# Wide operands in the first two feed-forwards of a four-layer transformer kernel, with a third of their weight splits on GpSimd

## The reference

```python
def conv_ffn(h, w_up, w_conv, w_down):
    gu = causal_dwconv(h @ w_up, w_conv)
    g, u = jnp.split(gu, 2, axis=-1)
    return (jax.nn.silu(g) * u) @ w_down
```

## Time and profile before

| | |
|---|---|
| median of three runs | 1244.94 us (1244.0 to 1245.01) |
| the profiled execution's own time | 1244.72 us |
| its span, first to last instruction | 1243.4 us |
| TensorE (PE) busy | 1228.2 us, 99% |
| VectorE (DVE) busy | 858.4 us, 69% |
| ScalarE (ACT) busy | 622.3 us, 50% |
| GpSimd (POOL) busy | 63.1 us, 5% |
| granted TensorE clock, mean | 0.999 |

### The profile page before, as it was taken

The page is one execution under the profiler, slowest core; times in us unless marked ns, Lnnn a source line. Parts: engine busy times, 40 slices in busy tenths (PEclk is TensorE's granted clock), DMA queues, the critical chain, the costliest instruction groups (busy, mean ns, idle before and its releaser), DMA issues.

```text
span 1243.4 us, 18327 instructions
## 1 busy us (share of the span) xinstructions
PE 1228.2 (99%) x7609; PEld 1085.7 (87%) x7609; DVE 858.4 (69%) x1126; ACT 622.3 (50%) x780; POOL 63.1 (5%) x84
## 2 busy tenths in 40 slices
PE   9999999999999999999999999999999999999997
PEld 8998999988877899988899888888889987888886
DVE  6656877646776787863678787776477567777744
ACT  6536655434556565543575635444326663644430
POOL 0000000000000000000006400000010001000000
PEclk9999999999999999999999999999999999999999
DMA  9654555554533445555443347455536341755530
GB/s 357 242 189 179 186 176 187 196 192 162 194 127 111 186 171 193 179 203 175 162 173 126 137 173 263 175 200 182 176 107 246 106 169 69 270 172 200 173 132 34
DMA packets 32658, 219.25 MB, mean 176 GB/s; under 512 B 3760, under 2 KB 4032, under 8 KB 7616
## 3 DMA queue, kind: packets, MB, share of 16 engines
q1 hardware_dynamic: 30848, 211.80, 47.8%
q0 software_dynamic: 1728, 6.29, 1.4%
HBM read 217.01 MB, written 1.05 MB: 175 GB/s over the span
## 4 chain that ended last, share of the span: by engine, by line
PE 94%; DVE 2%; ACT 2%; DMA 1%; POOL 1%; issue 0%; SPq 0%; DVEq 0%; POOLq 0%
PE ps L873 40%; PE ps L816 11%; PE ps L824 9%; PE ps L828 9%; PE ps L825 9%; PE ps L817 6%; PE ps L818 2%; PE ps L915 1%; PE ps L886 1%; PE ps L925 1%; PE ps L942 1%; DMA t<-in_rows 1%; PE ps L994 0%; DVE t L1413 0%; DMA t<-in_wts 0%; PE ps L1008 0%
## 5 line engine op out<-in xcount | busy, mean ns | idle before, releaser
L873 PE MATMUL ps<-t,t 128*128 128x512 f32 (+2 forms) x2280 | 541.9, 392 | 0.0
L1413 DVE TENSOR_TENSOR t<-t,t 128x2048 fp32r<-128x2048 f32 (+1 forms) x199 | 451.6, 2280 | 118.6 <-PE ps L873 101.5
L873 PEld LDWEIGHTS ps<-t,t 128*128 128x128 f32 x2280 | 417.1, 188 | 84.7 <-issue 1.4
L1117 ACT CAST t<-t 128x2048 fp32r<-128x2048 f32 (+1 forms) x199 | 376.1, 1899 | 226.2 <-PE ps L873 120.7
L824 PE MATMUL ps<-t,t 128*128 128x256 f32 x1024 | 257.7, 284 | 0.0
L825 PE MATMUL ps<-t,t 128*128 128x256 f32 x1024 | 256.6, 283 | 0.0
L816 PE MATMUL ps<-t,t 128*128 128x512 f32 x560 | 201.1, 398 | 0.0
L824 PEld LDWEIGHTS ps<-t,t 128*128 128x128 f32 x1024 | 196.4, 192 | 0.4 <-issue 0.2
L825 PEld LDWEIGHTS ps<-t,t 128*128 128x128 f32 x1024 | 196.4, 192 | 0.2
L817 PE MATMUL ps<-t,t 128*128 128x256 f32 x640 | 166.6, 281 | 0.0
L828 PE MATMUL ps<-t,t 128*128 128x256 f32 x1024 | 164.6, 283 | 0.0
(11 more groups left out here) (201 smaller groups left out, 788.1 us busy)
## 6 DMA issues: line engine op xcount, KB each, us to landing
t<-in_wts SPq DMA_DIRECT2D x195, 1024.0 KB, 4.9
t<-in_rows POOLq DMA_DIRECT2D x12, 512.0 KB, 4.4
t<-in_wts SPq DMA_DIRECT2D x4, 512.0 KB, 5.2
t<-in_wts SPq DMA_DIRECT2D x2, 768.0 KB, 5.0
t<-in_x_in SPq DMA_DIRECT2D x2, 512.0 KB, 4.0
out<-t SPq DMA_DIRECT2D x4, 256.0 KB, 2.1
t<-in_rows SPq DMA_DIRECT2D x2, 256.0 KB, 6.5
t<-in_cst SPq DMA_DIRECT2D x1, 448.0 KB, 13.5
```

The lines of the kernel that those rows point to most:

```text
L873: ins = mm(ps[:, t_bank(stage, t, j), 0:c1 - c0], a, w[:, k, c0:c1], start=kt == 0 and part == 0, stop=kt == KTS[stage] - 1 and part == 2)
L1117: copy(wh[:, k, 0:w], wraw[:, r, 0:w]).then_inc(s_hi, 1)
L1413: tt(wl[:, k, 0:w], wraw[:, r, 0:w], wh[:, h, 0:w].bitcast(F32), ALU.subtract).then_inc(s_lo, 1)
```

## The change

The first two feed-forwards get the wide form too. Three things go with it.

1. `WIDE` now holds all four feed-forwards: 16 matmuls a block, two banks an output, and the matmuls of n+2 wait for `s_wide` of n.
2. The halves are not joined by one reduction. ScalarE copies the half that comes from the low activations into SBUF (`low_half`: 128 x 512 into `XN[:, 1, ...]`, two halves used in turn), and VectorE adds the other half from PSUM to it, in place (`tensor_tensor`). All taps for n >= 2 then read the joined output from SBUF instead of PSUM. ScalarE's copy waits for the matmuls and for the taps of n-2; VectorE's sum for the copy; ScalarE's first tap for the sum.
3. The low split of every third chunk of ffn0 and ffn1 (six in each: places 2, 5, 8, 11, 14, 17 of the 20) is made by GpSimd instead of VectorE (`pool_splits`), with a semaphore of its own; TensorE and SyncE wait for it where they waited for VectorE's.

The order of a step changes with it. Before, step n was: taps n, pump, SiLU or product n. Now it is: copy and sum n, SiLU or product of n-1, pump, taps n.

In the diff the first `lo` is VectorE's and the last GpSimd's; the lines with `s_half_out` and `return` stand in VectorE's `wide_sum`.

```diff
-WIDE = ("ffn2", "ffn3")
+WIDE = HEADED
+def pool_splits(i):
+    return PLAN[i][0] in ("ffn0", "ffn1") and CHUNKS[PLAN[i][0]].index(i) % 3 == 2
...
         for m in done:
             name = "product" if m % 2 else "silu"
-            out += [("conv", q, m)] * (q < 2) + [("wide", q, m)] * (q >= 2 and m > 1) + [("pump",)] * (m == n) + [(name, q, m // 2)]
+            if q >= 2:
+                out += [("wide", q, m)] * (m > 1) + [("pump",)] * (m == n) + [(name, q, m // 2)]
+        if q < 2:
+            late = lambda m: ("product" if m % 2 else "silu", q, m // 2)
+            if n == 2:
+                out += [("conv", q, 0), ("conv", q, 1), late(0), late(1)]
+            out += [("wide", q, n)] + [late(n - 1)] * (n > 2) + [("pump",), ("conv", q, n)] + [late(n)] * (n == 21)
...
+    def lo_ready(i):
+        pooled = sum(pool_splits(n) for n in range(i + 1))
+        return (s_lop, pooled) if pool_splits(i) else (s_lo, split_at(i) - pooled)
...
+    def conv_in(q, n):
+        return ps[:, f_bank(f"ffn{q}", n), :] if n < 2 else XN[:, 1, half_of(n % 2)]
...
         def ffn_conv(q, n):
-            act.wait_ge(*f_done(f"ffn{q}", n))
+            act.wait_ge(*(f_done(f"ffn{q}", n) if n < 2 else wide_at(q, n)))
...
+        def low_half(q, n):
+            bank = f_bank(f"ffn{q}", n)
+            act.wait_ge(*f_done(f"ffn{q}", n))
+            if n >= 4:
+                act.wait_ge(s_cv, 22 * q + n - 1)
+            copy(conv_in(q, n).rearrange("p (a s) -> p a s", a=2), ps[:, bank:bank + 2, S:2 * S]).then_inc(s_half_out, 1)
...
         def lo(i):
-            if i >= len(PLAN):
+            if i >= len(PLAN) or pool_splits(i):
...
             dve.wait_ge(*f_done(stage, n))
+            if q < 2:
+                u = conv_in(q, n).rearrange("p (a s) -> p a s", a=2)
+                dve.wait_ge(s_half_out, 20 * q + n - 1)
+                tt(u, ps[:, bank:bank + 2, 0:S], u, ALU.add).then_inc(s_wide, 1)
+                return
...
+        def lo(i):
+            if i >= len(PLAN) or not pool_splits(i):
+                return
+            w, r, h, k = PLAN[i][5] * PLAN[i][6], i % NRAW, i % NHI, i % NLO
+            pool.wait_ge(*used(i - NLO))
+            pool.wait_ge(s_hi, split_at(i))
+            tt(wl[:, k, 0:w], wraw[:, r, 0:w], wh[:, h, 0:w].bitcast(F32), ALU.subtract).then_inc(s_lop, 1)
```

More of the change, by code:

```diff
@@ L507, in program @@
     s_tap, s_cv, s_silu = sem("s_ffn_tap"), sem("s_ffn_conv"), sem("s_ffn_silu")
-    s_wide = sem("s_ffn_wide_summed")
+    s_wide, s_half_out = sem("s_ffn_wide_summed"), sem("s_ffn_wide_half_copied")
     s_headc, s_headt = sem("s_head_copied"), sem("s_head_turned")
@@ L575, in wide_at @@
     def wide_at(q, n):
-        return s_wide, 20 * (q - 2) + n - 1
+        return s_wide, 20 * q + n - 1
     def ffn_read(q, n):
+        if n > 1:
+            return wide_at(q, n)
         if q < 2:
             return s_cv, 22 * q + n + 1
-        if n > 1:
-            return wide_at(q, n)
         return (s_pr if n % 2 else s_silu), 11 * q + n // 2 + 1
@@ L599, in f_bank @@
             return 2 + n
-        return 4 + (2 * (n % 2) if stage in WIDE else (n - 2) % 4)
+        return 4 + 2 * (n % 2)
     def f_bank_free(stage, n):
@@ L610, in f_bank_free @@
         q = int(stage[3])
[L611 to L615, removed]
+        return (s_xl, xl_at(NORM_BEFORE[q], n - 2, 1)) if n < 4 else wide_at(q, n - 2)
     def f_done(stage, n):
@@ L718, in turn_bank_free @@
         if b in (2, 4, 6):
-            return ffn_read(b // 2 - 1, 20 + (bank - 4) // 2 if b == 6 else bank + 14)
+            return ffn_read(b // 2 - 1, 20 + (bank - 4) // 2)
         if b == 5:
@@ L807, in f_block @@
             if blk == 0:
-                pe.wait_ge(s_lo, split_at(i))
+                pe.wait_ge(*lo_ready(i))
                 pe.wait_ge(*f_bank_free(stage, n))
@@ L1140, in ffn_conv @@
             k, dst = n // 2 % 2, yu if n % 2 else yg
+            act.wait_ge(*(f_done(f"ffn{q}", n) if n < 2 else wide_at(q, n)))
+            if n >= 4:
+                act.wait_ge(*((s_hl, 11 * q + n // 2 - 1) if n % 2 else (s_silu, 11 * q + n // 2 - 1)))
+            first_tap(dst[:, k, :], conv_in(q, n), "ffn_w_conv",
+                      132 * q + 22 * (n % 2) + 2 * (n // 2) + 2 * 44, s_tap)
+        def low_half(q, n):
+            bank = f_bank(f"ffn{q}", n)
             act.wait_ge(*f_done(f"ffn{q}", n))
             if n >= 4:
-                act.wait_ge(*((s_hl, 11 * q + n // 2 - 1) if n % 2 else (s_silu, 11 * q + n // 2 - 1)))
-            first_tap(dst[:, k, :], ps[:, f_bank(f"ffn{q}", n), :], "ffn_w_conv",
-                      132 * q + 22 * (n % 2) + 2 * (n // 2) + 2 * 44, s_tap)
+                act.wait_ge(s_cv, 22 * q + n - 1)
+            copy(conv_in(q, n).rearrange("p (a s) -> p a s", a=2), ps[:, bank:bank + 2, S:2 * S]).then_inc(s_half_out, 1)
         def silu(q, m):
@@ L1378, in act_program @@
                 copy(pair(Mh, m), prod[:, m % 2, :]).then_inc(s_sc_h, 1)
+            elif kind == "wide" and k[0] < 2:
+                low_half(*k)
             elif kind == "conv":
@@ L1837, in fill @@
             memset(dst, value).then_inc(done, 1)
+        nxt = [NLO]
         for s in STEPS:
             kind, k = s[0], s[1:]
-            if kind == "rows":
+            if kind in ("pump", "pump_lo"):
+                lo(nxt[0])
+                nxt[0] += 1
+            elif kind == "rows":
                 b = k[0]
@@ L1906, in load @@
                 sp.wait_ge(s_hi, split_at(i - NRAW))
-                sp.wait_ge(s_lo, split_at(i - NRAW))
+                sp.wait_ge(*lo_ready(i - NRAW))
             dma(wraw[:, k, 0:w], wts[i, :, 0:w]).then_inc(s_raw[k], 16)
```

4 lines of the change are left out of this document (2 added, 2 removed).

## The result

The changed kernel takes 1284.54 us, median of four runs (1283.8 to 1285.15), against 1244.85 us for the kernel before in the same comparison (1244.0 to 1245.01): a ratio of 1.0321, 95% interval 1.0308 to 1.0333, or 39.7 us more where 24.4 were forecast. The time lies beyond the upper end of the range, 1282.0. The profiled execution took 1283.8 us with a span of 1282.5.

A forecast was written before the change was run, and what follows sets the result against it. TensorE, busy 99% of the span, was taken as the bound; GpSimd's holds on VectorE would make each feed-forward 12.2 us longer, twice that 24.4: 1244.72 + 24.4 + 0.22 = 1269.3 us, range 1239.5 to 1282.

The forecast's parts named there:

- Part 1, the matmuls: ffn0 and ffn1 matmuls: wide form gives ffn2's 113.24 us, 2.38 us off each, 4.76 in all; alone 1240.2 us.
- Part 2, joins and taps, and the loop: VectorE and ScalarE in ffn0 and ffn1: two outputs take 11.31 us against TensorE's 11.29; no reserve, but it fits.
- Part 3, who is held, and when: GpSimd's splits come up behind VectorE's low split and hold its SBUF-reading taps, costing the loop 3.1 us each.
- Rivals B and C: GpSimd's splits: no hold worth the name, 1240.2 us, chance 0.23; or holds half covered, 1253 us, chance 0.11.
- Part 3, how long GpSimd needs: GpSimd's 128 x 2048 split: 3.58 us estimated from shorter instructions, upper end 4.16; hold taken as 3.5 us.
- the prediction's own sum: One feed-forward: first sum at 9.9 us, 17 outputs in 96.1, five holds 15.5; matmuls end at 127.8 instead of 115.62.
- The start of ffn0: VectorE's third head split ends 4.6 us after ffn0's first matmul, and the first sum starts at 9.9 us.
- Rival D, the clock: Gaps of up to 3.5 us in TensorE's work lower its clock, adding 14 us: 1283 us, chance 0.08.
- A: Likeliest case: GpSimd's splits hold VectorE's taps and so TensorE, 1269.3 us, own range 1256 to 1280; chance 0.58.

The follow-up runs named there:

- no_pool: Changed kernel with all low splits back on VectorE, wide matmuls, copy and sum kept: 1241.51 us, ratio 0.9977 to the kernel before.
- reduce: Changed kernel without GpSimd splits, halves joined by one VectorE reduction instead of ScalarE's copy and VectorE's sum: 1247.36 us, ratio 1.0025 to the kernel before.
- narrow_pool: Kernel before the change, narrow matmuls kept, with only the twelve low splits moved to GpSimd: 1244.32 us, ratio 0.9998.
- fill: Changed kernel with 22 unused 256-column matmuls before the bank wait of outputs 5, 11 and 17 in both feed-forwards: 1279.77 us, ratio 1.0281 to the kernel before.
- phase: Changed kernel with GpSimd's splits at places 5, 7, 9, 11, 13, 15, started only after earlier taps end: 1253.45 us, ratio 1.0069 to the kernel before.
- pieces: Changed kernel with each GpSimd split cut into four instructions of 512 columns: 1278.26 us, one run.
- half: Changed kernel with GpSimd making only columns 0 to 1023 of its twelve splits and VectorE the other 1024: 1257.09 us, one run.
- write_only: Changed kernel with all low splits on VectorE and four GpSimd memsets of unused memory in place of each GpSimd split: 1242.68 us, one run.

## Why the prediction fell short

**Part 1, the matmuls.** Right. no_pool's ffn0 takes 113.24 us, as ffn2 does.

**Part 2, joins and taps, and the loop.** Right: 11.33 us measured for two outputs against 11.31, from rows of other stages. The even output takes 6.36 us and the odd one 4.97, where 6.35 and 4.96 were reckoned. That it gains nothing on TensorE was right too (reduce). One term was too large: the prediction puts the sum of output 19 96.1 us behind the first, and in no_pool it is 223.88 - 128.80 = 95.1. The 17 outputs begin with output 2, in whose step no product is made.

**Part 3, who is held, and when.** Right. Instructions with two inputs in SBUF are held for GpSimd's whole instruction and those out of PSUM are not (narrow_pool); GpSimd is released by ScalarE's weight cast, comes up behind VectorE's low split and takes the taps; the cover is 0.4 us in the mean (fill). In two of the twelve cases the matmuls of i-4 release GpSimd last, and not the cast. The row at 690.66 in the earlier trace rows could not show that an input in PSUM spares VectorE the hold, since that instruction starts ahead of GpSimd's; narrow_pool shows it. Rivals B and C are out: nothing lets VectorE through, and it takes another release to get the hold into a wait (phase).

**Part 3, how long GpSimd needs.** This is the step that failed. The estimate was 3.58 us and the hold 3.5; measured are 4.60 and 4.4, beyond even the upper end from rows, 4.16. The Trainium skill's 4497 ns for such an instruction (GPSIMD Engine Reference, Elementwise — side-by-side cycle accounting) was within 3% of it. In the prediction's own sum 0.9 us more per hold is 4.5 a feed-forward, 9.0 of the 15.2 us that were missing. The rows that it was drawn from are of other forms. The 1.04 us of the earlier trace rows is L1868, which multiplies two inputs that are both repeated across the output (one a block used four times, the other a single value for 128 columns); L1879, with one full input and one repeated, takes 1.04 us too where it waits for nothing. The split subtracts two full inputs and writes fp32r: 1.29 us at the shortest for 512 columns (pieces), 2.44 for 1024 (half), 4.60 for 2048. That is 2.2 to 2.3 us for each further 1024 columns, where the estimate's 0.82 us for 496 is 1.7. "Same shape" was too coarse a match for a price. Which difference it is, the second full input, the subtraction or the output's type, no run separates.

**The start of ffn0.** The first sum was expected 9.9 us after the first matmul; it comes at 129.58 - 118.74 = 10.8, and in no_pool at 9.6. GpSimd's split of the head (4.85 us at 117.35) holds VectorE's third one there (5.25 us at 119.11), which ends 5.6 us after the first matmul where 4.6 were reckoned with. That is the same mis-sized term once more, 0.9 us a feed-forward. With the three terms put right the prediction's own sum gives 10.8 + 95.1 + 0.7 + 5 x 4.0 = 126.6 for the last sum and 132.3 for ffn0. fill has 132.5.

**Rival D, the clock.** It was given 0.08 as a case of its own, with a price of 14 us, and nothing in the sum. It happened, as part of A, and filling the six long gaps gave 4.8 us back (fill). Both choices were wrong in form: the gaps were A's own consequence, so the clock belonged to A's sum, and its price should have been cut by what VectorE holds up anyway. TensorE's idle time in ffn0, 14.1 us, lies within the 12 to 15 that the prediction named, but by luck: some 6 us of work more were lost at the low clock.

**Before ffn0.** 1.5 us were in no step. Near the kernel's start, where neither the splits on GpSimd nor the wide matmuls have begun, VectorE waits longer for the second part of the gain rows:
```profile
11.17 1.42 DVE L1482 SCALAR_TENSOR_TENSOR t<-t,t,t 128x512 f32<-128x512 f32 x2 [2.05 <-DMA t<-in_rows]
```
In the kernel before the same instruction starts at 10.15, after a wait of 1.13. It is late in every profile with the wide form (11.17 to 11.64; 11.61 in no_pool), and not in narrow_pool, where ffn0 begins at 116.58. So it comes with the wide form and not with GpSimd. The first matmul of ffn0 starts 2.0 us later in no_pool than before (119.17), more than the 1.3 us by which no_pool misses Part 1's 1240.2; that the late start is those 1.3 us is likely, not shown. Why the transfer lands later stays open; no run here changed it alone.

The account of the 39.7 us: -4.8 by Part 1, +1.3 for what no_pool misses, +38.3 for the holds, +4.8 for the clock: 39.6. It closes by construction, since its last three terms are differences between times; the better test is the sum above, 132.3 us against 132.5. Of the 15.2 us that the prediction missed, 9.0 are GpSimd's duration, 1.8 its share in the head, 4.8 the clock and 1.3 the late start, less 2.0 for the term that was too large: 14.9.

What would have put the forecast right before any run: a wider bound for GpSimd's duration. Three short instructions of different forms carried one term that was multiplied by ten. Where a term is that heavy and its row is not of the same form, the Trainium skill's figure deserved to be an end of the range at least: with 4497 ns the forecast was some 1278, and an upper end moved by the same 9 us, from 1282 to 1291, would have held 1284.5.

## What to carry to other kernels

Work moved to GpSimd from VectorE costs GpSimd's whole duration less whatever wait of that engine it falls into, and what it frees is worth only what that engine ends last with. So look for the instructions that can be held (two inputs in SBUF) and for who stands behind them: here the same splits cost nothing where a late product was held and VectorE had time in reserve, 12 us where they fell into a wait, and 43 where the tensor engine stood behind. Before a loop is given an extra wait, take the reserve of that loop (here none per output, 11.33 us against 11.29, and 2.2 us of head start); and where the wait will be long enough to leave TensorE idle, count the clock in the same sum.

## What the runs showed of the hardware that was not expected

- GpSimd's subtraction of two full 128-partition inputs takes 1.29 us at the shortest for 512 columns, 2.44 for 1024 and 4.60 for 2048; a multiplication with one or both inputs repeated takes 1.04 for 512.
- GpSimd that only writes (four memsets, 4.00 us) holds none of VectorE's instructions.
- A wait of 2.85 us before a matmul was followed by 5.9 us at a granted clock of 0.50, 1.2 GHz. The length of the wait alone does not decide: the clock fell behind waits of 1.91 and 2.04 us in ffn1 of half, and not behind 2.01 and 2.04 us in its ffn0, nor behind 2.88 and 2.58 us before output 14 in fill. The slow stretches lose 6.4 us of work in ffn0 of the changed kernel alone, and filling the six long gaps gave back 4.8 us in the whole kernel.
- With the wide form a DMA of gain rows lands 1.0 to 1.5 us later near the start. TensorE's granted clock between 10 and 20 us is 0.83 in the changed kernel and in no_pool and 1.00 in the kernel before, but it is 1.00 in fill, half and write_only too, where the rows are as late: the low clock there is not what delays them. The cause was not found.
